# A two-layer MLA and Conformer MoE block: query copies on ScalarE, rotary sums on Pool, a negated maximum, and another order of the conv loads

## The chip, the cores and the metric

The kernel runs on one core of a Trainium2 chip. The metric is the device time of one execution in microseconds (us); with several executions it is their median. All data are float32 but for a few one-hot tables in bfloat16.

## The reference

Layer 0 mixes 512 latent tokens and 256 context tokens by latent attention with 16 heads, layer 1 by a Conformer convolution; each is followed by a mixture of 64 experts, 6 per token, plus a shared expert. Cut to what matters here:

```python
# layer 0: queries, 16 heads of 64 + 32 dims; the last 32 are rotated
q = (rmsnorm(h @ wq_a, q_norm) @ wq_b).reshape(B, L, 16, 96)
q_pe = v * cos + rot(v) * sin            # v = q[..., 64:]
s = einsum('bqhd,bkhd->bhqk', q, k) * 96 ** -0.5   # 768 keys
p = softmax(s)
x = x + g1 * (einsum('bhqk,bkhd->bqhd', p, v) @ wo)
x = x + g2 * moe(modulate(rmsnorm(x)))
# layer 1: conv
u = h @ pw1_w + pw1_b                    # 1024 -> 2048
u = a * sigmoid(g)                       # then 31 taps, layernorm, silu
x = x + g1 * (u @ pw2_w + pw2_b)
x = x + g2 * moe(modulate(rmsnorm(x)))
# both layers: shift, scale and gate of "modulate" are silu(c) @ mod_w
```

## The kernel before

The program is written out by hand for the engines, each with its own stream; semaphores are the only order between them. Tensors are held feature-major: 128 features on the partitions, tokens along the row. SBUF has a ring of four slots of 24 KB a partition for weights (`ring`), a tile `hT` of the same 24 KB for normalised activations, and `work`.

**Attention.** Heads go in 8 pairs (`m`), each pair in 8 blocks of 128 queries (`n`, with `i8 = n % 8`). For a block PE makes the scores (`scores`, L906) two blocks ahead of use, DVE takes their maximum over 768 keys (L1309) and multiplies it by minus the scale (L1311), ScalarE takes the exponential with that bias (L735) and sums it, DVE divides (L1315, L1317), PE transposes the result (`turn`, L916), and ScalarE (L353) and DVE (L355) copy it out of PSUM. DVE's copy of block n comes ahead of the division of block n+1. After the eighth block PE multiplies with V (L941). Between, PE projects the next pair in six parts (`project`): keys (L885), the two heads' queries (L889, parts 2 and 3 in blocks 2 and 3), values (L894, parts 4 and 5 in blocks 4 and 5). Part 4 reuses the PSUM bank of part 2, part 5 that of part 3. DVE empties the query banks in `q_out`, in blocks 3 and 4: a copy of 64 rows (L1296), two rotary products (L1297, L1298) and their sum (L1300). The order on DVE is that of the loop at L1320: divide, maximum of the next block, `q_out`, copy, and then, in five of eight blocks (1, 3, 4, 6 and 7), one mod block (L1228), which is a dot product of a row of the modulation weights, in `ring`, with silu(c), in `small`. Pool has no work during the attention: it clears a tile and issues two transfers of zeros to `y_rows` ahead of it (L537 to L541).

**MoE.** SP loads each expert's weights into a ring slot as soon as that slot's last user is done (`refill_up`, `refill_down`; `dn_ps` counts finished down products, the four shared ones first). One block of an expert with over 128 tokens is run as an extra block behind the 64 experts, once a layer, with its own load (L429). Then Pool gathers the results, 24 gathers of 128 rows of 4 KB (L530) into six buffers, and DVE adds them into the accumulator (L1535, `comb_used` counts). PE transposes the sums (L1143), the next norm follows, and the conv starts with PE's products with `pw1` (L1169). `pw1` lies in ring slots 0, 1 and two thirds of 2, `pw2` behind it. SP issues both loads at L453 and L454, once 20 gathered tiles are added.

## Time and profile before

| what | value |
|---|---|
| median of three timed runs | 2224.37 us (2222.91 to 2260.46) |
| profiled execution, its own time | 2243.39 us |
| its span, first to last instruction | 2241.0 us |
| mean granted TensorE clock | 0.932 of full |
| busy share PE, DVE, ScalarE, Pool | 83, 40, 20, 15% |
| attention | 134 to 445 us |
| MoE layer 0, experts | 540 to 1170 us |
| gathers and norm | 1170 to 1256 us |
| conv | 1256 to 1495 us |
| MoE layer 1 to the end | 1495 to 2241 us |

Busy shares are averages over stages of different kinds: the experts' stages wait for weights, the attention is a loop over three engines. What an edit is worth is read in its own stage, from the wait that ends last there. The page lists an engine's idle time with what ended it; a wait for several semaphores is put down to the last.

### The profile page before, as it was taken

How to read it: one execution, taken by the hardware profiler on the slowest of the kernel's cores; microseconds unless marked ns; L12 is line 12 of the kernel's file. 1: busy time of each engine (PE TensorE's matmuls, PEld its weight loads, DVE VectorE, ACT ScalarE, POOL GpSimd, SP SyncE). 2: the span in 40 equal slices, each digit the busy share in tenths (PEclk: the TensorE clock that was granted, in tenths of full speed). 3: DMA queues.
4: the chain of work that ended last, by engine and by line, in shares of the span. 5: the costliest groups of instructions: out<-in, count | busy, mean ns of one | idle time of the engine just before them, and what ended most of it. 6: DMA issues, size and time to landing. Idle time of an engine off the chain costs nothing.

```text
span 2241.0 us, 30677 instructions
## 1 busy us (share of the span) xinstructions
PE 1849.6 (83%) x9312; PEld 958.0 (43%) x9313; DVE 901.8 (40%) x1635; ACT 450.8 (20%) x807; POOL 346.2 (15%) x540
## 2 busy tenths in 40 slices
PE   5988989797999788887980898788989789988952
PEld 3444545444554444444440343344544445444521
DVE  1567777755422222222215489435322212221235
ACT  4133433303111111111110355321111111110102
POOL 0000000001011111111104078101111111111132
PEclk9999999998999999999995799799999999999985
DMA  9497221446699999999969200036899999999954
GB/s 391 162 366 309 76 76 38 188 150 277 243 409 398 408 393 397 397 402 394 390 215 358 101 1 0 0 128 246 308 399 406 395 394 411 400 398 392 379 192 161
DMA packets 94528, 624.56 MB, mean 279 GB/s; under 512 B 16000, under 2 KB 16128, under 8 KB 56704
## 3 DMA queue, kind: packets, MB, share of 16 engines
q1 hardware_dynamic: 43488, 499.18, 55.7%
q0 software_dynamic: 26112, 79.72, 9.8%
q10 hardware_dynamic: 24864, 44.84, 5.6%
q8 instruction: 36, 0.59, 0.1%
q14 instruction: 28, 0.23, 0.0%
HBM read 562.86 MB, written 76.28 MB: 285 GB/s over the span
## 4 chain that ended last, share of the span: by engine, by line
PE 54%; DMA 23%; DVE 9%; issue 4%; POOL 3%; ACT 2%; DVEq 0%; SPq 0%; ACTq 0%; POOLq 0%
DMA ring<-in 20%; PE PS L959 10%; PE PS L965 9%; PE PS L1169 5%; PE PS L972 5%; PE PS L986 4%; PE PS L997 3%; PE PS L1187 3%; PE PS L950 3%; PE PS L889 2%; POOL work L530 2%; PE PS L906 2%; PE PS L941 2%; PE PS L916 2%; DVE ring L1228 1%
## 5 line engine op out<-in xcount | busy, mean ns | idle before, releaser
L965 PE MATMUL PS<-ring,work 128*64 128x256 f32 x3360 | 414.1, 402 | 111.0 <-issue 108.2
L965 PEld LDWEIGHTS PS<-ring,work 128*64 128x64 f32 x3360 | 246.6, 144 | 254.3 <-issue 157.7
L1358 DVE TENSOR_TENSOR work<-work,PS 64x256 f32<-64x256 f32 x105 | 44.4, 423 | 518.5 <-ACT work L610 515.3
L972 PE MATMUL PS<-ring,work 128*64 128x512 f32 x840 | 203.3, 605 | 1.2 <-ACT work L636 0.7
L959 PE MATMUL PS<-ring,work 128*128 128x512 f32 x400 | 182.6, 611 | 19.5 <-issue 10.8
L1363 DVE COPY work<-PS 128x1024 f32<-128x1024 f32 x128 | 156.7, 1225 | 12.2 <-PE PS L997 2.2
L482 POOL COPY col_i<-idx 128x1 int32 (+1 forms) x128 | 23.2, 181 | 840.2 <-PE PS L997 825.5
L488 POOL DMA_INDIRECT work<-h_rows,col_i x128 | 124.7, 975 | 169.9 <-issue 169.9
L997 PE MATMUL PS<-cst,work 128*128 128x128 f32 x1040 | 140.8, 278 | 0.0
L610 ACT ACTIVATE work<-PS 64x256 f32<-64x256 f32 x105 | 39.5, 376 | 481.0 <-PE PS L965 481.0
L997 PEld LDWEIGHTS PS<-cst,work 128*128 128x128 f32 x1040 | 113.4, 141 | 53.4 <-issue 53.4
L1369 DVE COPY work<-PS 128x256 f32<-128x256 f32 x136 | 57.7, 424 | 181.2 <-PE PS L992 181.2
L959 PEld LDWEIGHTS PS<-ring,work 128*128 128x128 f32 x400 | 75.8, 194 | 110.5 <-issue 110.5
L986 PE MATMUL PS<-ring,work 128*128 128x512 f32 x264 | 119.2, 594 | 1.0 <-DVE work L1528 1.0
L554 POOL TENSOR_TENSOR work<-work 128x512 f32<-128x512 f32 x80 | 104.8, 1314 | 92.4 <-ACT work L760 83.0
L636 ACT ACTIVATE work<-PS 128x512 f32<-128x512 f32 x105 | 62.7, 597 | 268.9 <-PE PS L972 232.3
L1169 PE MATMUL PS<-hT,ring 128*128 128x512 f32 x256 | 114.1, 605 | 1.7 <-ACT hT L593 1.7
L1228 DVE SCALAR_TENSOR_TENSOR ring<-ring,small 128x1024 f32<-128x1024 f32 x80 | 95.5, 1219 | 36.4 <-DMA ring<-in 36.0
L1143 PE MATMUL PS<-cst,work 128*128 128x128 f32 x64 | 15.2, 389 | 110.4 <-DVE work L1535 110.4
L906 PE MATMUL PS<-work,hT 96*128 96x512 f32 (+1 forms) x256 | 96.4, 500 | 0.0
L1356 DVE TENSOR_TENSOR work<-work,PS 128x256 f32<-128x256 f32 x31 | 13.0, 419 | 197.3 <-ACT work L608 197.3
L972 PEld LDWEIGHTS PS<-ring,work 128*64 128x64 f32 x840 | 51.1, 136 | 79.2 <-issue 77.3
(233 smaller groups left out, 2145.8 us busy)
## 6 DMA issues: line engine op xcount, KB each, us to landing
ring<-in SPq DMA_DIRECT2D x155, 2048.0 KB, 17.2
ring<-in SPq DMA_DIRECT2D x130, 1024.0 KB, 17.7
y_rows<-sq POOLq DMA_DIRECT2D x2, 14336.0 KB, 61.4
y_rows<-work ACTq DMA_DIRECT2D x210, 128.0 KB, 9.1
ring<-in SPq DMA_DIRECT2D x3, 4096.0 KB, 14.7
y_rows<-work ACTq DMA_DIRECT2D x46, 256.0 KB, 9.8
ring<-in SPq DMA_DIRECT2D x2, 3072.0 KB, 12.4
h_rows<-work ACTq DMA_DIRECT2D x8, 512.0 KB, 15.8
```

The lines of the kernel that those rows point to most:

```text
L488: pool.indirect_dma_start(out=xg[n][0:p], out_offset=None, in_=h_rows[i], in_offset=bass.IndirectOffsetOnAxis(ap=col_i[0:p, n:n + 1], axis=0),
L554: nc.gpsimd.tensor_tensor(side[c % 2], before, tap_prod[n % 4], ALU.add).then_inc(side_add, 1)
L906: last = mm(bank(2 * (n % 2), 2)[:, c0:c0 + w], qT[m % 2][q][0:96, t * 128:(t + 1) * 128], kT[m % 2][q][0:96, c0:c0 + w], start=True, stop ...
L950: last = mm(bank(n % 2), wo_sb[:, c, n * 128:(n + 1) * 128], oT[:, c, :], start=(c == 0), stop=(c == DC - 1))
L959: last = mm(bank(6), lhs(c), w13(s)[:, :, c, :], start=(c == 0), stop=(c == DC - 1))
L965: last = mm(bank(6)[64 * q:64 * q + 64, 0:F], lhs(c)[:, 0:64], w13(s)[:, q, c, :], start=(c == 0), stop=(c == DC - 1), tile_position=(0, 6 ...
L972: last = mm(bank(4)[64 * q:64 * q + 64, :], actT[par][:, kk, 0:64], w2(s)[:, kk, q * 512:(q + 1) * 512], start=(kk == 0), stop=(kk == 1), ...
L986: last = mm(bank(4 + half), actT[par][:, kk, :], w2(s)[:, kk, half * 512:(half + 1) * 512], start=(kk == 0), stop=(kk == 1))
L997: last = tr(bank(1, 2)[:, c * 128:(c + 1) * 128], xg[par][:, c * 128:(c + 1) * 128], ident)
L1169: last = mm(bank(2 * (c % 2) + half), pw1_sb[:, kk, half * D + c * 128:half * D + (c + 1) * 128], hM[:, kk, :], start=(kk == 0), stop=(kk ...
L1228: last = V.scalar_tensor_tensor(mod_tile[at][:, j, :], mod_tile[at][:, j, :], 1.0, cs_row, ALU.mult, ALU.mult, accum_out=mod[i][:, part, c ...
L1363: V.tensor_copy(xgT[par].rearrange("p c t -> p (c t)"), bank(1, 2)).then_inc(xgT_ev, 1)
```

## The change

- `q_out` on DVE keeps only the two rotary products (new lines L1321 and L1322). The copy of the 64 plain rows goes to ScalarE (`q_copy`), after the exponentials of blocks 3 and 4, and multiplies by the softmax scale. The sum of the products goes to Pool, 16 times, and counts `q_ev`. The table of cosines and sines for queries is multiplied by the scale, so the exponential has none.
- The value projections wait for the products (`q_rope`) and the copy (`q_cp`), no longer for the sum; the scores wait for copy and sum. In the first pair ScalarE makes both query copies ahead of the value copies.
- The maximum is reduced with `negate=True` into the bias itself; the multiplication and its semaphore go.
- `pw1` is loaded in three parts: its share of slot 1 once expert 60 is done, that of slot 2 once expert 62 is done, that of slot 0, and then `pw2`, once all 24 gathers have landed. The extra expert block's weights go into `hT` and wait for no ring slot, in both layers.

```diff
+        SPARE = RING
+        def slot_ap(s):
+            return hT[:, :] if s == SPARE else ring[:, s * SLOT:(s + 1) * SLOT]
...
                     with nc.sync.Fori(0, many) as j:
-                        sp.wait_ge(m["dn_ps"], TT + E - 3)
                         sp.wait_ge(m["t_dn"], j + 1)
                         e = nc.sync.value_load(unit_i[0:1, ds(j, 1)], min_val=0, max_val=E - 1)
-                        expert(ds(e, 1), slot_of(E - 4), m["t_w"])
+                        expert(ds(e, 1), SPARE, m["t_w"])
...
-            sp.wait_ge(comb_used, TT * K - 4)
-            sp.dma_start(pw1_sb.rearrange("p c f -> p (c f)"), pw1).then_inc(pw_in, 16)
+            def load_pw1(k0, k1):
+                sp.dma_start(ring[:, k0 * 2 * D:k1 * 2 * D], pw1[:, k0 * 2 * D:k1 * 2 * D]).then_inc(pw_in, 16)
+            sp.wait_ge(M[0]["dn_ps"], TT + E - 3)
+            load_pw1(3, 6)
+            sp.wait_ge(M[0]["dn_ps"], TT + E - 1)
+            load_pw1(6, 8)
+            for n in range(6):
+                sp.wait_ge(comb_in[n], 16 * (TT * K // 6))
+            load_pw1(0, 3)
             sp.dma_start(pw2_sb.rearrange("p c f -> p (c f)"), pw2).then_inc(pw2_in, 16)
...
+            for n in range(H):
+                pool.wait_ge(q_rope, n + 1)
+                nc.gpsimd.tensor_tensor(qT[n // 2 % 2][n % 2][64:96, :], rope_t[0][64:96, :], rope_t[1][64:96, :], ALU.add).then_inc(q_ev, 1)
             moe(0)
...
+            def q_copy(m, q):
+                a.wait_ge(pj_ps, 6 * m + 3 + q)
+                A(qT[m % 2][q][0:64, :], bank(7 if q == 0 else 6)[0:64, :], ACT.Copy, scale=SM_SCALE).then_inc(q_cp, 1)
...
-                A(P[n % 2], bank(2 * (n % 2), 2)[:, 0:KEYS], ACT.Exp, bias=smx[:, n % 4, 1:2], scale=SM_SCALE,
+                A(P[n % 2], bank(2 * (n % 2), 2)[:, 0:KEYS], ACT.Exp, bias=smx[:, n % 4, 1:2],
                   accum_out=smx[:, n % 4, 2:3]).then_inc(exp_rdy, 1)
...
+                if m + 1 < NPAIR and i8 in (3, 4):
+                    q_copy(m + 1, i8 - 3)
...
-                elif part == 4:
-                    pe.wait_ge(q_ev, 2 * m + 1)
-                elif part == 5:
-                    pe.wait_ge(q_ev, 2 * m + 2)
+                elif part >= 4:
+                    pe.wait_ge(q_rope, 2 * m + part - 3)
+                    pe.wait_ge(q_cp, 2 * m + part - 3)
...
                 dve.wait_ge(pj_ps, 6 * m + 3 + q)
                 dve.wait_ge(q_ev, 2 * m + q)
-                dst = qT[m % 2][q]
-                V.tensor_copy(dst[0:64, :], b[0:64, :])
                 V.tensor_tensor(rope_t[0][64:96, :], b[64:96, :], k("rope")[64:96, :], ALU.mult)
                 V.tensor_tensor(rope_t[1][64:96, :], b[96:128, :], k("rope")[96:128, :], ALU.mult).then_inc(q_rope, 1)
-                dve.wait_ge(q_rope, 2 * m + q + 1)
-                V.tensor_tensor(dst[64:96, :], rope_t[0][64:96, :], rope_t[1][64:96, :], ALU.add).then_inc(q_ev, 1)
...
-                V.tensor_reduce(smx[:, n % 4, 0:1], bank(2 * (n % 2), 2)[:, 0:KEYS], AX.X, ALU.max).then_inc(max_rdy, 1)
-                dve.wait_ge(max_rdy, n + 1)
-                V.tensor_scalar(smx[:, n % 4, 1:2], smx[:, n % 4, 0:1], -SM_SCALE, None, ALU.mult).then_inc(nmax_rdy, 1)
+                V.tensor_reduce(smx[:, n % 4, 1:2], bank(2 * (n % 2), 2)[:, 0:KEYS], AX.X, ALU.max, negate=True).then_inc(nmax_rdy, 1)
```

The order on DVE in block 4 of the first pair, before: from the maximum of block 5 to the division of block 5 (`smx` holds maxima and sums, `PS` is PSUM, `hT` the queries, `ring` the products, P and the modulation weights).

```order
L1309 TENSOR_REDUCE smx<-PS 128x1 [waits p_rdy,s_ps]
L1311 TENSOR_SCALAR smx<-smx 128x1 [waits max_rdy]
L1296 COPY hT<-PS 64x512 [waits q_ev,pj_ps]
L1297 TENSOR_TENSOR ring<-PS,cst 32x512
L1298 TENSOR_TENSOR ring<-PS,cst 32x512
L1300 TENSOR_TENSOR hT<-ring 32x512 [waits q_rope]
L355 COPY work<-PS 128x2x128 [waits pT_ps]
L1228 SCALAR_TENSOR_TENSOR ring,mod<-ring,small 128x1024
L1315 RECIPROCAL smx<-smx 128x1 [waits exp_rdy]
L1317 TENSOR_SCALAR ring<-ring,smx 128x768 [waits den_rdy]
```

And with the change, where the file's later lines are some 20 further down:

```order
L1331 TENSOR_REDUCE smx<-PS 128x1 [waits p_rdy,s_ps]
L1321 TENSOR_TENSOR ring<-PS,cst 32x512 [waits q_ev,pj_ps]
L1322 TENSOR_TENSOR ring<-PS,cst 32x512
L360 COPY work<-PS 128x2x128 [waits pT_ps]
L1254 SCALAR_TENSOR_TENSOR ring,mod<-ring,small 128x1024
L1335 RECIPROCAL smx<-smx 128x1 [waits exp_rdy]
L1337 TENSOR_SCALAR ring<-ring,smx 128x768 [waits den_rdy]
```

Three instructions less stand between the maximum and the copy of P transposed; the mod block, which reads `ring` and `small`, is now the second instruction behind the last rotary product, whose semaphore starts Pool's sum.

SP's queue at the end of the first MoE layer, before: the extra block's two loads (ring), and the conv loads.

```order
L388 ISA
L388 DMA ring<-in 128x4096
L391 ISA
L391 DMA ring<-in 128x2048
L425 REGISTER_ALU
L425 COMPARE_AND_BRANCH
L424 UNCONDITIONAL_BRANCH
L453 DMA ring<-in 128x16384 [waits comb_used]
L454 DMA ring<-in 128x8192
```

And with the change:

```order
L393 ISA
L393 DMA hT<-in 128x4096
L396 ISA
L396 DMA hT<-in 128x2048
L430 REGISTER_ALU
L430 COMPARE_AND_BRANCH
L429 UNCONDITIONAL_BRANCH
L458 DMA ring<-in 128x6144 [waits dn_ps0]
L458 DMA ring<-in 128x4096 [waits dn_ps0]
L458 DMA ring<-in 128x6144 [waits comb_in3,comb_in4,comb_in2,comb_in5,comb_in1,comb_in0]
L467 DMA ring<-in 128x8192
```

The extra block's loads go to `hT`; `pw1` is split in three, and only its last part and `pw2` stand behind the wait for the gathers.

## Rows read from the trace of the kernel before

**Rows 1.** Busy time in two stretches: attention, end of the first MoE layer.
```profile
core 0: us, PE busy (x) PEld busy (x) DVE busy (x) ACT busy (x) POOL busy (x), PEclk, DMA share, GB/s
134.00:445.00 311.00, 269.92 (x1191) 154.99 (x1189) 230.35 (x470) 118.31 (x237) 0.00 (x0) 0.98 0.43 167
...
1170.00:1238.00 68.00, 4.96 (x14) 2.46 (x15) 31.60 (x26) 1.23 (x2) 27.13 (x25) 0.56 0.85 328
```

**Rows 2.** Chain of waits, attention: start, length, products with V of three pairs.
```profile
174.62 5.30 PE PS L941 x24
...
214.34 5.30 PE PS L941 x24
...
252.91 5.30 PE PS L941 x24
```

**Rows 3.** Stretches of 3 us, pair 3: the one of low clock.
```profile
283.00:286.00 3.00, 2.89 (x8) 1.89 (x9) 2.28 (x6) 1.75 (x4) 0.00 (x0) 0.55 0.00 0
```

**Rows 4.** Timeline, pair 2 between turn(4) and turn(7): start, length, engine, line.
```profile
239.22 0.68 DVE L1296 COPY hT<-PS 64x512 f32<-64x512 f32 x1
...
239.92 0.69 DVE L1297 TENSOR_TENSOR ring<-PS,cst 32x512 f32<-32x512 f32 x1
...
241.35 0.68 DVE L1300 TENSOR_TENSOR hT<-ring 32x512 f32<-32x512 f32 x1
242.07 0.42 DVE L355 COPY work<-PS 128x256 f32<-128x256 f32 x1
...
242.09 1.16 PE L894 MATMUL PS<-ring,work 128*128 128x128 f32 x8 [1.27 <-DVE hT L1300]
242.52 1.23 DVE L1228 SCALAR_TENSOR_TENSOR ring<-ring,small 128x1024 f32<-128x1024 f32 x1
...
244.54 0.88 PE L916 MATMUL PS<-cst,ring 128*128 128x128 f32 x6 [1.29 <-DVE ring L1317]
...
245.38 0.15 DVE L1311 TENSOR_SCALAR smx<-smx 128x1 f32<-128x1 f32 x1
...
250.74 0.88 PE L916 MATMUL PS<-cst,ring 128*128 128x128 f32 x6 [1.10 <-DVE ring L1317]
```

**Rows 5.** Lines L1576 and L554 (ns: shortest, median, longest), and Pool's run.
```profile
L1576 DVE TENSOR_TENSOR work<-work x8: 693/1673/1681, 1298.3 to 1411.8; 128x512 f32<-128x512 f32 x8
...
L554 POOL TENSOR_TENSOR work<-work x80: 1261/1272/1545, 1276.8 to 1409.2; 128x512 f32<-128x512 f32 x80
...
1295.49 5.57 POOL L554 TENSOR_TENSOR work<-work 128x512 f32<-128x512 f32 x4
```

**Rows 6.** Timeline, first pair: the wait ahead of its second V projection.
```profile
136.63 1.16 PE L894 MATMUL PS<-ring,work 128*128 128x128 f32 x8 [1.12 <-DVE hT L1300]
```

**Rows 7.** Timeline, last gathers of the first MoE layer and the conv loads.
```profile
1209.81 8.22 DVE L1535 SCALAR_TENSOR_TENSOR work<-work,small 128x1024 f32<-128x1024 f32 x6 [0.64 <-DMA work<-y_rows,row_i]
...
1212.22 1.07 POOL L530 DMA_INDIRECT work<-y_rows,row_i  x1 [0.30 <-issue]
1213.90 0.34 SPq L453 DMA_DIRECT2D ring<-in  x1
...
1235.84 1.28 DVE L1535 SCALAR_TENSOR_TENSOR work<-work,small 128x1024 f32<-128x1024 f32 x1 [17.81 <-DMA work<-y_rows,row_i]
...
1237.18 1.97 PE L1143 MATMUL PS<-cst,work 128*128 128x128 f32 x8 [62.14 <-DVE work L1535]
...
1256.82 5.46 PE L1169 MATMUL PS<-hT,ring 128*128 128x512 f32 x6 [1.72 <-ACT hT L593]
```

**Rows 8.** Line L530, all gathers of rows: issue to landing.
```profile
DMA to landing us min/median/max: 4.2/6.1/23.6
```

**Rows 9.** Timeline, second MoE layer: the same transposes.
```profile
2209.58 1.97 PE L1143 MATMUL PS<-cst,work 128*128 128x128 f32 x8 [48.28 <-DVE work L1535]
```

**Rows 10.** SP's queue: the last expert load and the extra block's.
```profile
1136.29 0.33 SPq L391 DMA_DIRECT2D ring<-in  x1
1143.89 0.35 SPq L388 DMA_DIRECT2D ring<-in  x1
```

More of the change, by code:

```diff
@@ L166, in build @@
         qT = [[hT[:, DC * T + (2 * a + b) * T:DC * T + (2 * a + b + 1) * T] for b in range(2)] for a in range(2)]
-        assert o[0] <= 12800
+        assert o[0] <= 12800 and DC * KEYS == SLOT
         hM = hT[:, 0:DC * T].rearrange("p (c t) -> p c t", c=DC)
@@ L220, in build @@
         rw_sb = hT[:, DC * T:DC * T + DC * E].rearrange("p (c e) -> p c e", c=DC)
+        SPARE = RING
+        def slot_ap(s):
+            return hT[:, :] if s == SPARE else ring[:, s * SLOT:(s + 1) * SLOT]
         def w13(s):
-            return ring[:, s * SLOT:s * SLOT + 2 * DC * F].rearrange("p (a c f) -> p a c f", a=2, c=DC)
+            return slot_ap(s)[:, 0:UP].rearrange("p (a c f) -> p a c f", a=2, c=DC)
         def w2(s):
-            return ring[:, s * SLOT + 2 * DC * F:(s + 1) * SLOT].rearrange("p (k d) -> p k d", k=2)
+            return slot_ap(s)[:, UP:SLOT].rearrange("p (k d) -> p k d", k=2)
         pw1_sb = ring[:, 0:DC * 2 * D].rearrange("p (c f) -> p c f", c=DC)
@@ L252, in build @@
         pj_ps, kv_ev, q_ev, q_rope = sem("pj_ps"), sem("kv_ev"), sem("q_ev"), sem("q_rope")
-        s_ps, max_rdy, nmax_rdy, exp_rdy, p_rdy, pT_ps, pT_act, pT_dve, o_ps, o_ev = (
-            sem(n) for n in ("s_ps", "max_rdy", "nmax_rdy", "exp_rdy", "p_rdy", "pT_ps", "pT_act", "pT_dve", "o_ps", "o_ev"))
+        s_ps, q_cp, nmax_rdy, exp_rdy, p_rdy, pT_ps, pT_act, pT_dve, o_ps, o_ev = (
+            sem(n) for n in ("s_ps", "q_cp", "nmax_rdy", "exp_rdy", "p_rdy", "pT_ps", "pT_act", "pT_dve", "o_ps", "o_ev"))
         wo_ps, wo_ev = sem("wo_ps"), sem("wo_ev")
@@ L386, in expert_up @@
                 def expert_up(e, s, done):
-                    sp.dma_start(ring[:, s * SLOT:s * SLOT + UP], exp_w[i, e, :, 0:UP].rearrange("o p n -> p (o n)")).then_inc(done, 16)
+                    sp.dma_start(slot_ap(s)[:, 0:UP], exp_w[i, e, :, 0:UP].rearrange("o p n -> p (o n)")).then_inc(done, 16)
                 def expert_down(e, s, done):
-                    sp.dma_start(ring[:, s * SLOT + UP:(s + 1) * SLOT], exp_w[i, e, :, UP:SLOT].rearrange("o p n -> p (o n)")).then_inc(done, 16)
+                    sp.dma_start(slot_ap(s)[:, UP:SLOT], exp_w[i, e, :, UP:SLOT].rearrange("o p n -> p (o n)")).then_inc(done, 16)
                 def expert(e, s, done):
@@ L726, in kv_out @@
                 last.then_inc(kv_ev, 1)
-            for part in (0, 1, 4, 5):
-                kv_out(0, part)
+            def q_copy(m, q):
+                a.wait_ge(pj_ps, 6 * m + 3 + q)
+                A(qT[m % 2][q][0:64, :], bank(7 if q == 0 else 6)[0:64, :], ACT.Copy, scale=SM_SCALE).then_inc(q_cp, 1)
+            kv_out(0, 0)
+            kv_out(0, 1)
+            q_copy(0, 0)
+            q_copy(0, 1)
+            kv_out(0, 4)
+            kv_out(0, 5)
             for n in range(NS):
@@ L901, in scores @@
                 pe.wait_ge(kv_ev, 4 * m + 2)
+                pe.wait_ge(q_cp, 2 * m + 1 + q)
                 pe.wait_ge(q_ev, 2 * m + 1 + q)
@@ L1130, in moe @@
                         pe.wait_ge(m["t_w"], j * 32 + 32)
-                        up_mm(lambda c: xgT[0][:, c, :], slot_of(E - 4)).then_inc(m["t_up"], 1)
+                        up_mm(lambda c: xgT[0][:, c, :], SPARE).then_inc(m["t_up"], 1)
                         pe.wait_ge(m["t_act"], j + 1)
@@ L1136, in moe @@
                         pe.wait_ge(m["y_ev"], TT + E)
-                        down_mm(0, slot_of(E - 4)).then_inc(m["t_dn"], 1)
+                        down_mm(0, SPARE).then_inc(m["t_dn"], 1)
                 pe.wait_ge(comb_used, TT * K + i * TT * K)
@@ L1150, in _ @@
             moe(0)
-            pe.wait_ge(pw_in, 16)
+            pe.wait_ge(pw_in, 48)
             def conv_taps(c):
@@ L1614, in constants @@
     cos, sin = np.cos(ang.astype(np.float32)), np.sin(ang.astype(np.float32)) * sign
-    put("rope", np.concatenate([cos, sin, cos, sin]))
+    put("rope", np.concatenate([cos, sin, cos * SM_SCALE, sin * SM_SCALE]))
     return c
```

## The prediction

> **What bounds the kernel now.** I read the chain that ended last first, since shares of busy time mix stages. Most of it is PE, and most of the transfers in it are expert weights, which the change leaves alone. So I look at two stretches only: the attention, where the chain runs over PE with short DVE pieces between, and the end of the first MoE layer.
>
> The table of stretches tells the two apart [rows 1]. In the attention, 134 to 445, PE is busy 269.92 of 311 us and DVE 230.35: neither fills it, so it is a loop of waits. In 1170 to 1238 PE is busy 4.96 of 68 us, while the DMA engines are at 0.85 of their time and move 328 GB/s: the stage waits for gathers.
>
> Pairs of heads are told apart by the starts of the product with V in the chain: 174.62, 214.34, 252.91, so 39.72 and 38.57 us [rows 2]. Every other pair holds some 3 us in which the granted clock is near the lower of its levels, as 0.55 in 283 to 286, after PE had waited twice [rows 3]; I take 38.57 as the undisturbed pair. Seven of the eight pairs also project the next pair and hold its two q_out calls.
>
> Inside a pair I follow turn (L916), which closes each block of 128 queries [rows 4]. In blocks 0 to 4 the projections keep PE full, and DVE waits for PE. After turn(4) it flips: DVE runs the second q_out (copy 239.22, first product 239.92, add 241.35), then the copy of P transposed at 242.07, a mod block at 242.52, and then the division. PE waits 1.27 us for the add before its last projection (242.09) and 1.29 us more before turn(5) at 244.54; turn(7) comes at 250.74.
>
> **The change part by part.** DVE's first q_out of a pair lies under four projection matmuls and is worth nothing. From the second goes the copy, 0.70 us from its start to the next start (239.22 to 239.92), and the add, 0.72 us (241.35 to 242.07) [rows 4]. The separate negation, 0.15 us long, stands between the maximum and the exponential or q_out; it goes as well: of it I count 0.1 us here. Together DVE reaches the copy of P transposed 1.5 us sooner. After turn(5) comes a block without a mod block, where the path is maximum, exponential, division, turn(6), and the negation is worth its 0.15 us [rows 4]. The two blocks behind it carry mod blocks and run round copy, mod block, division and turn; the negation is not in that loop, so nothing more. Sum without any new cost: 1.65 us a pair.
>
> ScalarE's new copies of 64x512 take about what the 64x512 copy takes on DVE, 0.68 us [rows 4]. Each stands behind the exponential of blocks 3 and 4 and ahead of a copy which waits for a turn behind the projection in any case; the projection that it reads is done before that turn. I cost it at nothing; were that cover gone, it is 0.68 us a call, and turn(5) would be late by it.
>
> The add on Pool is not in the trace. Its nearest row is Pool's 128x512 addition, 1.27 us, twice DVE's [rows 5]. Nobody waits for its result: the scores that read it stand in block 7, over 10 us later, and the projections now wait for the products and the copy. But it runs beside DVE, and a row speaks against that. DVE's L1576, an addition with both operands in SBUF, takes 0.693 us at its shortest and 1.673 at the median, and the first, at 1298.3, lies inside a run of Pool's additions [rows 5]: 0.98 us lost. The mod block L1228 also reads two SBUF tensors (ring and small), and in block 4 it is issued 0.45 us behind the copy that starts just as Pool starts. If it must wait for Pool's 1.27 us, it loses 1.27 - 0.45, some 0.9 us with the hand-over. In block 3 Pool is done before DVE has anything to issue.
>
> The bounds of this edit are thus 1.65 us (no wait) and 1.65 - 1.27 = 0.4 us (the whole addition lost). I take 1.65 - 0.9, rounded to 0.8 us a pair, since L1576 is the nearest row: same engine pair, same kinds of operands.
>
> The Trainium skill has a rule for it (SBUF — State Buffer, Who interferes with whom): a DVE instruction with two SBUF inputs and a GpSimd instruction that reads SBUF share a port pair, and the one that comes second is held for the whole of the other. By that rule it is 0.8 us a pair, without it 1.65; the trace agrees with the rule in L1576.
>
> Attention: 7 x 0.8 = 5.6 us. In the first pair the second V projection waited 1.12 us for the add until 136.63 [rows 6]; about 1.0 of it goes, as the products end 0.7 us sooner by the missing copy and the add is not waited for. The last pair has no projections; its three blocks without a mod block gain the negation, 3 x 0.15, some 0.4. Sum 7.0 us, bounds 4.2 and 13.0. PE's clock may gain or lose with the shorter gaps, the odd pairs' 1.1 us each; I leave that in the range.
>
> The reduction that negates is not in the trace. From below it can be what the reduction is now, which is my value: the same elements are read and one number written. From above see the third rival.
>
> The load order. Before, both conv weights are issued at 1213.90, when 20 of 24 gathered rows are added; the last gather was issued at 1212.22 [rows 7]. DVE is done with the others at 1209.81 + 8.22 = 1218.03 and then waits 17.81 us for that one gather, to 1235.84; PE starts at 1237.18. Any gather takes 6.1 us at the median to land, this one 23.6 [rows 8]: it shares the DMA engines with 12 MB. After the change nothing is issued until the gathers have landed, but for 5 MB of pw1 that go out when the experts 60 and 62 are done, at about 1144 and 1158, well before the first gather. So the last gather lands at 1212.22 + 1.07 + 6.1 = 1219.4, its addition takes 1.28, and PE starts at about 1220.8: 16.4 us sooner. The best case is DVE never waiting: 1218.03 + 1.34 = 1219.4, 17.8 us. The other end is the second layer, where no load stands behind the gathers: PE's idle time ahead of the same transposes is 48.28 us there and 62.14 here, so 13.9 us [rows 7, 9]. I take 16.
>
> Is the rest of the load in time? Slot 0's 3 MB and then pw2 are issued at 1219.4. At 328 GB/s [rows 1] 3 MB are 9.6 us, with 2 to 3 us of delay 1232. The first conv matmul stood at 1256.82 [rows 7], now about 1240.5: covered by 8 us. If the cover went because pw2 ran abreast, 7.3 MB at that rate land at 1242 to 1244, and it costs 2 to 3 us.
>
> SP's part in the tail: the extra block's weights now go into hT right behind expert 63's, at about 1136.6 and not 1143.89, and 3 MB of pw1 follow at 1143.9 [rows 10]. In this queue nothing stands behind them but each other; ScalarE's stores and Pool's last row gather run abreast. The gather is read only at 1160. I cost it at nothing.
>
> **Sum.** 7.0 + 16.0 = 23.0 us. The profiled execution took 2243.39 us for its span of 2241.0, so 2220.4 by its own time. It lies 0.9% above the timed median 2224.37, which is 1.4 above the lowest of the three; I carry the difference over to the median: 2201.4 us.
>
> **Rivals.** (a) Pool and DVE don't meet: 1.65 a pair, 11.6 + 1.4 = 13.0 us, 29 in all: 2195 us. For it: a 32-partition addition may be shorter than 1.27; against it the 0.98 us of L1576.
>
> (b) The early loads hold up the end of the first MoE layer. Expert 63's last MB (issued 1136.6) shares with 3 MB more, up to 9.6 us late against some slack, so 4; then the tail's gather and the last stores share with 5 MB of pw1, up to 9 more: 13 lost, 2214 us. For it: expert weights are still being issued at 1136, so the queues are not empty [rows 10]. Against it: the 5 MB are through by about 1166, ahead of the first gather.
>
> (c) Slower: the negated maximum takes a longer form. The price by blocks: three of eight blocks a pair are bound by DVE, all eight in the last pair, 7 x 3 + 8 = 29 reductions on the path. At twice the present length, 0.95 more each, that is 27.6 us lost against 23.0 won: 2229 us. It decides from 23.0 / 29 = 0.79 us extra a reduction. Nothing in the trace speaks for it but that no such row exists.
>
> (d) The loads change nothing: the last gather is late by itself, and only the 7 us of the attention stay, 2217 us. Against it: no gather of the second layer holds DVE more than about 1 us.
>
> **How the numbers follow.** The forecast 0.50, (a) 0.17, (b) 0.14, (c) 0.04, (d) 0.07, and 0.08 for what no row prices: the weight-bound MoE stages, which differ from one execution to the next (the three timed runs reach from 2222.91 to 2260.46). The range takes in (a) with four odd pairs freed of their clock dip and the best load case, 13.0 + 4.4 + 17.8 = 35, 2189, and 4 us of spread: 2185; above, (b) and (d) with a few us of spread: 2223. A change of 2%, 44.5 us, is about what a measurement of this kernel can tell from none. More than that to the good needs 2180, below the best case of every term: 0.07. Slower by over 2% needs (c) at well over double length or a disturbed stage: 0.03. Within 2%: 0.90.
>
> **What would show it.** In the profile after: pairs of about 37.8 us between V products; L1576-like lengthening of one mod block a pair, from 1.22 to about 2.1 us, in block 4 only; no wait of the V projection on DVE; the reduction still 0.95 us. At the first MoE layer's end PE's wait for the accumulation is shorter by 16 us, the last gather lands in about 6 us, and the first pw1 matmul waits for ScalarE, not for a transfer. Wrong: mod blocks unchanged and pairs of 36.9 say (a); PE waiting for expert 63 or for rows at 1150 to 1165 says (b); long reductions say (c); a DVE gap of over 10 us ahead of the last addition says (d).

## The result and the profile after

The changed kernel takes 2216.30 us, the median of 20 runs (2206.74 to 2220.51). The kernel before, run beside it, takes 2243.42 us over 20 runs (2217.74 to 2260.46), the three shown ahead of the prediction among them. The ratio is 0.9906, with a 95% interval of 0.988 to 0.9932: about 21 us faster, which by the bound of 2% counts as no change. The ratio leaves out a kernel's runs over 1.5% above its fastest; over all runs the medians lie 27.1 us apart and the means 23.7. The forecast time was 2201.4 us; the range (2185 to 2223) holds the result.

| | before | after |
|---|---|---|
| profiled execution, us | 2243.39 | 2219.18 |
| its span, us | 2241.0 | 2217.4 |
| last product with V of the attention starts | 437.40 | 426.59 |
| first MoE layer: PE starts on the gathered sums | 1237.18 | 1216.13 |
| second MoE layer: the same | 2209.58 | 2186.43 |
| spread of 20 runs, us | 42.7 | 13.8 |

So 10.8 us come from the attention, 10.2 more by the first MoE layer's end, and 2.1 between there and the second layer's end, which the change hardly touches.

The table of stretches for the changed kernel, after [rows 1] (us; then busy time and count for PE, PEld, DVE, ACT and POOL; PEclk, DMA share, GB/s):

```profile
134.00:445.00 311.00, 276.53 (x1213) 158.09 (x1212) 210.72 (x382) 127.21 (x253) 18.90 (x15) 0.98 0.43 167
1170.00:1218.00 48.00, 1.87 (x8) 1.57 (x8) 31.54 (x25) 0.20 (x1) 31.36 (x25) 0.51 0.82 289
```

DVE gave up 20 us of work in the attention, ScalarE took 9 and Pool 18.9. The wait for gathered rows is still the most idle stretch, now 48 us long.

The chain of waits, attention: start, length, the products with V of the first four pairs and the last two.

```profile
172.89 5.30 PE PS L967 x24
...
210.47 5.30 PE PS L967 x24
...
248.06 5.30 PE PS L967 x24
...
285.65 5.30 PE PS L967 x24
...
398.43 5.30 PE PS L967 x24
...
426.59 7.00 PE PS L967 x24
```

Every pair takes 37.59 us, where [rows 2] had 38.57 and 39.72 in turn. The 3 us of low clock of [rows 3], which began 9.6 us ahead of a product with V (292.58 in that trace), are gone; the stretch at that place of the pair now shows a granted clock of 1.00 (in the order of the table of stretches, PEclk behind POOL):

```profile
276.00:279.00 3.00, 1.52 (x8) 1.10 (x9) 2.67 (x6) 0.68 (x1) 0.00 (x0) 1.00 0.00 0
```

The timeline of pair 2 after the change, from the first block that sends work to Pool (3) to turn(5), against [rows 4] (start, length, engine, line, operation, tiles, count, and the wait before it):

```profile
230.33 1.26 POOL L557 TENSOR_TENSOR hT<-ring 32x512 f32<-32x512 f32 x1 [29.91 <-DVE ring L1322]
231.95 0.42 DVE L360 COPY work<-PS 128x256 f32<-128x256 f32 x1 [1.70 <-PE PS L942]
232.41 1.23 DVE L1254 SCALAR_TENSOR_TENSOR ring<-ring,small 128x1024 f32<-128x1024 f32 x1
...
236.70 0.42 DVE L360 COPY work<-PS 128x256 f32<-128x256 f32 x1
236.75 1.26 POOL L557 TENSOR_TENSOR hT<-ring 32x512 f32<-32x512 f32 x1 [5.16 <-DVE ring L1322]
236.78 1.10 PE L919 MATMUL PS<-ring,work 128*128 128x128 f32 x8
237.16 1.93 DVE L1254 SCALAR_TENSOR_TENSOR ring<-ring,small 128x1024 f32<-128x1024 f32 x1
239.21 0.62 DVE L1337 TENSOR_SCALAR ring<-ring,smx 128x768 f32<-128x768 f32 x1
239.74 0.95 DVE L1331 TENSOR_REDUCE smx<-PS 128x1 f32<-128x768 f32 x1
239.88 0.87 PE L942 MATMUL PS<-cst,ring 128*128 128x128 f32 x6 [2.00 <-DVE ring L1337]
```

In block 3 Pool is through by 231.59, before DVE starts, and the mod block takes 1.23 us. In block 4 the mod block is issued 0.41 us behind Pool's start and takes 1.93 us: 0.71 longer, with its end as if it had begun at 237.87, just ahead of Pool's end at 238.01. The V projection (L919) waits for nothing. The reduction that negates takes 0.95 us, as the plain one did.

The timeline at the end of the first MoE layer after the change, against [rows 7]: the last additions, SP's loads, the transposes, and the first conv matmul.

```profile
1213.40 2.67 DVE L1555 SCALAR_TENSOR_TENSOR work<-work,small 128x1024 f32<-128x1024 f32 x2 [0.41 <-DMA work<-y_rows,row_i]
1214.83 0.33 SPq L458 DMA_DIRECT2D ring<-in  x1
1215.21 0.43 SPq L467 DMA_DIRECT2D ring<-in  x1
1216.13 1.97 PE L1169 MATMUL PS<-cst,work 128*128 128x128 f32 x8 [48.30 <-DVE work L1555]
...
1235.95 2.90 PE L1195 MATMUL PS<-hT,ring 128*128 128x512 f32 x3 [1.72 <-ACT hT L609]
```

None of the additions from 1210 on waits longer than 0.64 us, PE waits 48.30 us and not 62.14, and the conv's first matmul waits for ScalarE, 1.72 us as before. The line of the gathers, after [rows 8]:

```profile
DMA to landing us min/median/max: 4.3/5.8/6.5
```

What the prediction did not price stands in the tail of the same layer (timeline of the changed kernel): ScalarE's copies of a result wait for the store of an earlier one, and PE for them.

```profile
1145.17 0.60 ACT L652 ACTIVATE work<-PS 128x512 f32<-128x512 f32 x1 [4.95 <-DMA y_rows<-work]
...
1149.84 0.60 ACT L652 ACTIVATE work<-PS 128x512 f32<-128x512 f32 x1 [1.45 <-DMA y_rows<-work]
...
1150.58 1.94 PE L998 MATMUL PS<-ring,work 128*64 128x512 f32 x8 [1.25 <-ACT work L652]
...
1158.43 0.60 ACT L652 ACTIVATE work<-PS 128x512 f32<-128x512 f32 x1 [7.99 <-DMA y_rows<-work]
```

Here the stores are under way together with 5 MB of `pw1`; whether that is the cause is tried below (e11).

### The profile page after: what moved, and what is told of

Read it like the earlier page. It is cut to its first block, busy times and chain, and to the rows that moved or that the text cites. A ratio compares the mean times of both kernels' runs of the same rounds, so it can differ in the third digit from the quotient of the medians.

```text
span 2217.4 us, 30694 instructions
## 1 busy us (share of the span) xinstructions
PE 1846.7 (83%) x9312; PEld 957.4 (43%) x9313; DVE 877.6 (40%) x1539; ACT 459.9 (21%) x823; POOL 371.9 (17%) x556
## 4 chain that ended last, share of the span: by engine, by line
PE 55%; DMA 22%; DVE 8%; issue 4%; POOL 3%; ACT 2%; ACTq 0%; DVEq 0%; SPq 0%; POOLq 0%
DMA ring<-in 20%; PE PS L985 10%; PE PS L991 9%; PE PS L1195 5%; PE PS L1012 5%; PE PS L998 4%; PE PS L1023 3%; POOL work L543 3%; PE PS L914 3%; PE PS L1213 3%; PE PS L976 3%; PE PS L967 2%; PE PS L942 2%; DMA y_rows<-work 2%; PE PS L932 2%
## 5 line engine op out<-in xcount | busy, mean ns | idle before, releaser
L991 PE MATMUL PS<-ring,work 128*64 128x256 f32 x3360 | 422.7, 409 | 113.9 <-issue 111.2
L985 PE MATMUL PS<-ring,work 128*128 128x512 f32 x368 | 163.4, 597 | 11.7 <-issue 7.8
L626 ACT ACTIVATE work<-PS 64x256 f32<-64x256 f32 x105 | 39.4, 375 | 491.3 <-PE PS L991 489.0
L1254 DVE SCALAR_TENSOR_TENSOR ring<-ring,small 128x1024 f32<-128x1024 f32 x80 | 100.6, 1281 | 36.4 <-DMA ring<-in 35.9
L1012 PE MATMUL PS<-ring,work 128*128 128x512 f32 x248 | 111.8, 594 | 0.0
L985 PEld LDWEIGHTS PS<-ring,work 128*128 128x128 f32 x368 | 68.2, 190 | 92.4 <-issue 92.4
L1169 PE MATMUL PS<-cst,work 128*128 128x128 f32 x64 | 14.9, 385 | 96.7 <-DVE work L1555 96.7
```

What stands on the lines that cost most here:

```text
L985: last = mm(bank(6), lhs(c), w13(s)[:, :, c, :], start=(c == 0), stop=(c == DC - 1))
L991: last = mm(bank(6)[64 * q:64 * q + 64, 0:F], lhs(c)[:, 0:64], w13(s)[:, q, c, :], start=(c == 0), stop=(c == DC - 1), tile_position=(0, 6 ...
L1012: last = mm(bank(4 + half), actT[par][:, kk, :], w2(s)[:, kk, half * 512:(half + 1) * 512], start=(kk == 0), stop=(kk == 1))
L1254: last = V.scalar_tensor_tensor(mod_tile[at][:, j, :], mod_tile[at][:, j, :], 1.0, cs_row, ALU.mult, ALU.mult, accum_out=mod[i][:, part, c ...
```

## The experiments

For each kernel I read three stretches of its timeline: pair to pair in the attention; the tail, from the up products of the next-to-last expert of the first layer to the first gather's issue; and the gather stage, from there to PE's transposes. In the profiled executions, in us:

| kernel | pairs | tail | gather stage | slowest gather |
|---|---|---|---|---|
| before | 38.6 to 39.7 | 34.7 | 57.8 | 23.6 |
| after | 37.59 | 36.1 | 44.0 | 6.5 |
| changed kernel again (e14) | 37.59 | 40.3 | 40.9 | 6.8 |
| loads alone (e1) | 38.6 to 40.2 | 38.5 | 41.3 | 6.7 |
| attention alone (e2) | 37.59 | 34.6 | 39.9 | 6.7 |
| later `pw1` parts (e11) | 37.6 to 38.7 | 35.4 | 44.6 | 6.8 |
| before, loads at 18 added (e12) | 38.6 to 40.1 | 34.7 | 70.7 | 35.4 |
| before, loads at 24 added (e13) | 38.6 to 40.3 | 34.7 | 40.2 | 6.5 |

In the second layer of all these kernels, with no load near, the tail is 34.6 to 34.9 and the gather stage 40.1 to 44.7. So the gather stage by itself differs by some 4 us from one execution to the next, and the tail hardly at all.

**The loads alone (e1).** The kernel before, with the load order and the extra block in `hT` of the change, and nothing of the attention.

```diff
-                        sp.wait_ge(m["dn_ps"], TT + E - 3)
...
-                        expert(ds(e, 1), slot_of(E - 4), m["t_w"])
+                        expert(ds(e, 1), SPARE, m["t_w"])
...
-            sp.wait_ge(comb_used, TT * K - 4)
-            sp.dma_start(pw1_sb.rearrange("p c f -> p (c f)"), pw1).then_inc(pw_in, 16)
...
+            sp.wait_ge(M[0]["dn_ps"], TT + E - 3)
+            load_pw1(3, 6)
+            sp.wait_ge(M[0]["dn_ps"], TT + E - 1)
+            load_pw1(6, 8)
+            for n in range(6):
+                sp.wait_ge(comb_in[n], 16 * (TT * K // 6))
+            load_pw1(0, 3)
```

> The load order alone, on the kernel before (pw1 in three parts, the extra block's weights in hT). My theory: the attention stays at pairs of 38.6 and 39.7 us; no gather lands later than about 7 us; PE's idle time ahead of the transposes of the first MoE layer falls from 62 to about 48 us, of which up to 1.5 us is given back before it, because ScalarE's stores and the pw1 parts share the DMA engines. Sum 12 to 14 us faster than before. Rival: the load order carries the whole 21 us and the attention's gain is eaten by the weight-bound experts: then this run is 20 us or more faster. Second rival: the early parts cost as much as they bring: within 4 us of before.

Measured: 2228.80 us, median of 12 (2220.62 to 2237.40), against 2234.74 of the kernel before: ratio 0.9977 (0.9949 to 1.0006). The profile shows the 16 us shorter wait, yet the median moves by some 5 us. A gain that a profile shows in full and the runs show in part needed another theory.

**The attention alone (e2).** The changed kernel with the loads and ring slots of before.

```diff
-            sp.wait_ge(M[0]["dn_ps"], TT + E - 3)
-            load_pw1(3, 6)
-            sp.wait_ge(M[0]["dn_ps"], TT + E - 1)
-            load_pw1(6, 8)
...
+            sp.wait_ge(comb_used, TT * K - 4)
+            sp.dma_start(pw1_sb.rearrange("p c f -> p (c f)"), pw1).then_inc(pw_in, 16)
```

> The attention's edits alone, with the loads as before. My theory: pairs of 37.6 us without a clock dip, the last product with V 10 to 11 us sooner; the last gather of the first MoE layer still waits 17 to 24 us behind pw1 and pw2. Of the 10.8 us the experts' stage keeps about 2, so 8 to 9 us faster than before. Rival: the experts' stage is bound by its weights and absorbs all of it: within 2 us of before.

Measured: median 2218.61 us of 12, ratio 0.994 (0.990 to 0.9979), and runs from 2208.19 to 2248.88, so more than the 8 to 9 us expected. In the profiled one, at 2208.25, the wait that the change is meant to remove isn't there, though this kernel has the old loads. Its timeline, the last gather's issue, the loads, the transposes:

```profile
1199.16 1.07 POOL L531 DMA_INDIRECT work<-y_rows,row_i  x1 [0.30 <-issue]
...
1201.22 0.34 SPq L454 DMA_DIRECT2D ring<-in  x1
...
1206.81 1.97 PE L1157 MATMUL PS<-cst,work 128*128 128x128 f32 x8 [44.23 <-DVE work L1543]
```

The loads are issued 0.99 us behind the end of the last gather's issue, where [rows 7] had 1213.90 - 1213.29 = 0.61 us. The new theory: the kernel before is a mixture. In some executions the loads catch the last gather (it lands some 17 us late), in others it gets away. Its own 20 runs fit: twelve lie at 2242.96 or above, with a mean of 2248, eight at 2236.26 or below, with a mean of 2225. The gap between the two groups isn't always there: of the 23 runs of the kernel before that stand beside e1 and e2, five lie in it (2236.53 to 2242.26). So the time of a single run does not tell its kind.

**Loads a little earlier, and behind the gathers (e12, e13).** The kernel before with one number changed, so that its loads should catch the gathers always, or never.

```diff
-            sp.wait_ge(comb_used, TT * K - 4)
+            sp.wait_ge(comb_used, TT * K - 6)
```

(e12; e13 has `TT * K`.)

> The kernel before with one number changed: pw1 and pw2 are issued when 18 gathered tiles are added, not 20. My theory now: before is a mixture; when the loads are issued, the last gather is either already in the DMA queues or stands behind 8 to 12 MB, and that costs 16 to 18 us. With 18, two or three gathers are still to be issued, so every execution pays: no run below about 2238 us, a median 15 us above the lower runs of before, the longest gather 20 us or more in every profile. Rival: the slow runs of before come from something else in the chip; then this kernel has the same spread as before, 2220 to 2255.

> The kernel before with one number changed: pw1 and pw2 are issued when all 24 gathered tiles are added. No gather can stand behind them, so by my theory no run is slow: PE's transposes 40 to 44 us behind the first gather in every execution. pw1, now whole at that point, lands 24 us later, some 4 us after the first conv matmul could start, so it costs about 4 us against the lower runs of before: all runs in 2222 to 2235 us, the median 5 to 8 us below the median of before. Rival as in the run with 18: the spread stays at 30 us.

Measured: e12 takes 2252.14 us, median of 10, all between 2248.04 and 2259.47; ratio 1.0091 (1.0054 to 1.0127). Its timeline: the loads, the last gather's issue, and the last three additions, which wait for one gather each.

```profile
1214.08 0.34 SPq L453 DMA_DIRECT2D ring<-in  x1
...
1215.18 1.08 POOL L530 DMA_INDIRECT work<-y_rows,row_i  x1 [0.30 <-issue]
...
1235.66 1.28 DVE L1535 SCALAR_TENSOR_TENSOR work<-work,small 128x1024 f32<-128x1024 f32 x1 [17.07 <-DMA work<-y_rows,row_i]
1247.87 1.29 DVE L1535 SCALAR_TENSOR_TENSOR work<-work,small 128x1024 f32<-128x1024 f32 x1 [10.92 <-DMA work<-y_rows,row_i]
1250.57 1.28 DVE L1535 SCALAR_TENSOR_TENSOR work<-work,small 128x1024 f32<-128x1024 f32 x1 [1.42 <-DMA work<-y_rows,row_i]
...
1251.91 1.97 PE L1143 MATMUL PS<-cst,work 128*128 128x128 f32 x8 [74.97 <-DVE work L1535]
```

e13 takes 2228.99 us, median of 12, all between 2224.02 and 2235.97; ratio 0.9948 (0.9914 to 0.9982). Its timeline: the transposes, and the first conv matmul with its weight load, which waits for the transfer of `pw1`.

```profile
1222.92 1.97 PE L1143 MATMUL PS<-cst,work 128*128 128x128 f32 x8 [44.53 <-DVE work L1535]
...
1246.58 0.50 PEld L1169 LDWEIGHTS PS<-hT,ring 128*128 128x128 f32 x2 [6.09 <-DMA ring<-in]
1246.58 3.78 PE L1169 MATMUL PS<-hT,ring 128*128 128x512 f32 x4 [5.79 <-ACT hT L593]
```

The matmul waits 5.79 us and not 1.72, so it is 4.1 us late. One number moves all runs to the long side or all to the short one, and the spread falls to 11.4 and 12.0 us, where the kernel before, run beside them, has 39.1. So it is the order of loads and gathers that makes the spread. How many gathers a long run of the kernel before has caught isn't shown: one such execution has a trace, with one caught, and e12 catches three.

**The changed kernel again, and its early parts later (e14, e11).** e14 is the changed kernel once more. e11 issues both early parts of `pw1` only when all experts' down products are done.

```diff
-            sp.wait_ge(M[0]["dn_ps"], TT + E - 3)
+            sp.wait_ge(M[0]["dn_ps"], TT + E)
             load_pw1(3, 6)
-            sp.wait_ge(M[0]["dn_ps"], TT + E - 1)
             load_pw1(6, 8)
```

> The changed kernel once more, beside the next run on one chip. By my theory its ratio to before depends on how many executions of before caught the last gather: 0.988 to 0.994, its own runs within 15 us; pairs of 37.59 us; 36 to 39 us from the last two experts to the first gather. Rival: the pairs or that stretch differ from one execution to the next as much as between the kernels.

> The changed kernel with pw1's two early parts issued once the last of the 64 experts is done, and nothing else. If these parts hold up ScalarE's stores and the extra block, the stretch from the last two experts to the first gather falls to 34.6 to 35.7 us, 2 to 4 us less than in the changed kernel, and so does the median. Rival: the 36 to 39 us come from the extra block's weights being issued 7 us sooner, which is still so here; then the stretch stays at 36 or more.

Measured: e14 2212.68 us (2205.55 to 2215.42, 6 runs), e11 2211.36 us (2207.38 to 2220.86, 6 runs). The tail of e14 is longer than the 36 to 39 us expected. It falls from 40.3 to 35.4 us, nearly what it is without early parts: they cost it 5 us in that execution. The extra block's weights still go out early in e11, so it isn't they that hold the tail up. The timeline of e14 shows where:

```profile
1140.83 0.60 ACT L652 ACTIVATE work<-PS 128x512 f32<-128x512 f32 x1 [5.49 <-DMA y_rows<-work]
...
1147.50 3.68 PE L998 MATMUL PS<-ring,work 128*64 128x512 f32 x8 [2.50 <-ACT work L652]
...
1154.46 0.60 ACT L652 ACTIVATE work<-PS 128x512 f32<-128x512 f32 x1 [7.10 <-DMA y_rows<-work]
```

The time does not follow: the medians differ by 1.3 us, within both spreads. In e11's profile the gather stage takes 44.6 us, where the changed kernel's two executions have 44.0 and 40.9, and three pairs of its attention have a stretch of low clock (38.3 to 38.7 us). Whether the 5 MB, then nearer to the gathers, make them longer, I can't say: the second layer's stage reaches 44.7 with nothing beside it. Tail and gather stage together take 80.0 us in e11, and 80.1 and 81.2 in the changed kernel's two executions. All ten executions with parts issued ahead of the gathers have 78.1 to 81.2, the two without them and without a caught gather (e2, e13) 74.5 and 74.9. That looks as if moving the parts later only moved the loss; but the second layers, with no load near, reach from 74.6 to 79.6. So the hold-up is real in the tail; what it costs in the end stays open.

**The sum back on DVE (e6).**

```diff
-            for n in range(H):
-                pool.wait_ge(q_rope, n + 1)
-                nc.gpsimd.tensor_tensor(qT[n // 2 % 2][n % 2][64:96, :], rope_t[0][64:96, :], rope_t[1][64:96, :], ALU.add).then_inc(q_ev, 1)
...
+                dve.wait_ge(q_rope, 2 * m + q + 1)
+                V.tensor_tensor(qT[m % 2][q][64:96, :], rope_t[0][64:96, :], rope_t[1][64:96, :], ALU.add).then_inc(q_ev, 1)
```

> The changed kernel with the rotary sum back on DVE, behind the two products; Pool has none. DVE does the sum itself, 0.72 us, but its mod block in block 4 no longer waits for Pool, 0.71 us: the two cancel, pairs of 37.6 us again. Rival: handing the sum to Pool is worth its 0.72 us in full, and the pair is 38.3 us here; or, if the wait for the port is more than it looks, below 37.4.

Measured: one run, 2207.26 us, and pairs of 37.59 us, the same within a hundredth or two. Its timeline in block 4:

```profile
233.53 0.68 DVE L1321 TENSOR_TENSOR hT<-ring 32x512 f32<-32x512 f32 x1
234.24 0.42 DVE L360 COPY work<-PS 128x256 f32<-128x256 f32 x1
234.70 1.23 DVE L1251 SCALAR_TENSOR_TENSOR ring<-ring,small 128x1024 f32<-128x1024 f32 x1
...
236.72 0.87 PE L939 MATMUL PS<-cst,ring 128*128 128x128 f32 x6 [2.01 <-DVE ring L1336]
```

DVE spends 0.71 us on the sum, to the next start, and the mod block is 0.70 us shorter. The move to Pool is worth nothing.

**The sum on Pool twice (e5).** The second is issued behind the first and writes the same; the scores, and DVE's next pair of products, wait for both.

```diff
+                pool.wait_ge(q_ev, 2 * n + 1)
+                nc.gpsimd.tensor_tensor(qT[n // 2 % 2][n % 2][64:96, :], rope_t[0][64:96, :], rope_t[1][64:96, :], ALU.add).then_inc(q_ev, 1)
```

> The changed kernel with Pool's sum made twice (the second into the same rows, behind the first). If the mod block of block 4 waits for Pool, it now waits for both: about 3.2 us long, or 1.9 us and then the division long, and turn(5) comes about 1.3 us later; pairs of 38.9 us for 37.6. Rival: the 1.93 us are not Pool's; then the mod block stays at 1.93 and the pair at 37.6.

Measured: one run, 2230.14 us. Four of the six pairs take 40.5 us, two 39.8 and 39.5. The timeline in block 4:

```profile
239.42 1.26 POOL L557 TENSOR_TENSOR hT<-ring 32x512 f32<-32x512 f32 x1 [4.20 <-DVE ring L1324]
239.82 1.93 DVE L1256 SCALAR_TENSOR_TENSOR ring<-ring,small 128x1024 f32<-128x1024 f32 x1
240.75 2.12 POOL L559 TENSOR_TENSOR hT<-ring 32x512 f32<-32x512 f32 x1
...
241.88 1.42 DVE L1339 TENSOR_SCALAR ring<-ring,smx 128x768 f32<-128x768 f32 x1
...
243.35 1.54 PE L944 MATMUL PS<-cst,ring 128*128 128x128 f32 x6 [2.80 <-DVE ring L1339]
```

The two engines hold each other in turn: Pool's first the mod block (+0.7 us), the mod block Pool's second (2.12 for 1.26), that one the division (1.42 for 0.62). Nothing else differs, so this is the meeting of the two engines. The pairs lost 2.9 us and not the 1.3 expected. Counted from the last product with V, turn(5) comes 1.2 us later than in the changed kernel, as expected. The rest goes with the clock: the transposes behind the division take 1.54 us and not 0.87, and from 244 to 248 us the granted clock is 0.50, where the changed kernel has 1.00.

**The negation back (e7).**

```diff
-                V.tensor_reduce(smx[:, n % 4, 1:2], bank(2 * (n % 2), 2)[:, 0:KEYS], AX.X, ALU.max, negate=True).then_inc(nmax_rdy, 1)
+                link(V.tensor_reduce(smx[:, n % 4, 0:1], bank(2 * (n % 2), 2)[:, 0:KEYS], AX.X, ALU.max))
+                V.tensor_scalar(smx[:, n % 4, 1:2], smx[:, n % 4, 0:1], -1.0, None, ALU.mult).then_inc(nmax_rdy, 1)
```

> The changed kernel with the maximum negated by an instruction of its own again (by -1, the scale being in the queries). By my sum it is worth 0.1 us in block 4 and 0.15 in block 5: pairs of 37.84 us, and no difference in the last pair, where before and the changed kernel took 28.1 us each. Rival: it is worth 0.15 in every block that DVE bounds, 38.2 us a pair.

Measured: one run, 2221.41 us. Undisturbed pairs take 37.98 us, so 0.39 more, where I had counted 0.25; the last pair 28.8 and not 28.1. In three pairs a stretch of low clock is back (38.6 to 39.4 us). The line of the negation:

```profile
L1332 DVE TENSOR_SCALAR smx<-smx x64: 153/154/154, 137.5 to 426.5; 128x1 f32<-128x1 f32 x64
```

**Mod blocks elsewhere (e3, e4).** What binds block 4 on DVE is the mod block; the first blocks of a pair are bound by PE. e3 moves the one of block 4 to block 2, beside none there; e4 puts them in blocks 0, 1, 2 (two) and 3.

```diff
-                for b in range(n * ATTN_BLOCKS // NS, (n + 1) * ATTN_BLOCKS // NS):
+                BEFORE = (0, 0, 1, 2, 3, 3, 3, 4, 5)
+                for b in range(5 * m + BEFORE[i8], 5 * m + BEFORE[i8 + 1]):
```

(e4: `(0, 1, 2, 4, 5, 5, 5, 5, 5)`.)

> The changed kernel with one mod block a pair moved from block 4 to block 2 (same number a pair). If the 1.93 us of the mod block in block 4 is a wait for Pool's sum (port contention), all mod blocks now take 1.22 us, since Pool's sum meets only copies out of PSUM, and turn(5) comes 1.9 us sooner: 1.2 for the mod block itself, 0.7 for the lost wait; pairs of 35.7 us, the attention 13 us shorter, 10 to 13 us in all. Rival: the lengthening belongs to block 4 whatever runs there; then the division that now follows the copy is long (its 128x768 product over 1.3 us for 0.62), and a pair gains 1.2 us, not 1.9.

> The changed kernel with the five mod blocks of a pair in blocks 0, 1, 2, 2 and 3, where PE is full and DVE waits. Beyond the run with one moved block, turn(7) also comes about 0.5 us sooner (the loop of copy, mod block, division and turn, 3.27 us, gives way to that of maximum, exponential and division, about 2.8). Pairs of 35.2 us, the attention 16 to 17 us shorter than in the changed kernel, 2200 us in all or a little over. Rival: the second mod block of block 2 or the one of block 0 makes DVE late for turn(2) or turn(1); then a pair stays at 35.7 us or more and this run is no better than the one with one moved block.

Measured: e3 2206.76 us (4 runs, 2203.94 to 2210.04), ratio 0.9864 (0.9803 to 0.9925), pairs of 36.19. Half a microsecond of what I expected is missing, and its timeline in block 4 shows it:

```profile
231.77 1.26 POOL L557 TENSOR_TENSOR hT<-ring 32x512 f32<-32x512 f32 x1 [4.24 <-DVE ring L1322]
...
232.38 1.07 DVE L1337 TENSOR_SCALAR ring<-ring,smx 128x768 f32<-128x768 f32 x1
```

With the mod block gone, the division meets Pool's sum and takes 1.07 us for 0.62. e4: 2210.13 us (6 runs), pairs of 36.77 and a last pair of 30.8 instead of 28.2, where pairs of 35.2 were expected: the rival came true, and this is no better than e3. I put it down to the two mod blocks in one block, above all where nothing is projected; that was not tried by itself, and the last pair also has 6 us at a granted clock of 0.50 to 0.55 (408 to 414) ahead of its product with V.

**Two mod blocks moved (e10).** Mod blocks in blocks 0, 1, 2, 3 and 7, with e11's later parts.

```diff
+                BEFORE = (0, 1, 2, 3, 4, 4, 4, 4, 5)
```

> The changed kernel with the mod blocks of a pair in blocks 0, 1, 2, 3 and 7, and with pw1's two early parts issued once the last of the 64 experts is done, under the extra block. From the runs so far: a pair is 36.2 us with block 4 free of a mod block; with block 6 free too turn(7) comes 0.5 us sooner, 35.7 us a pair. From the last two experts to the first gather it took 34.6 us with the late loads and 36.1 to 39.1 with the early ones; here 34.6 to 35.5, since the 5 MB pass in the 15 us of the extra block. Transposes 40 to 44 us behind the first gather. In all about 12 to 16 us faster than the changed kernel, 2201 to 2205 us. Rival: the loads collide with the extra block's own store or with the first gathers, and the gathers' stage grows by 5 us or more.

Measured: 2197.93 us, median of 6 (2195.01 to 2200.18), against 2238.82 of the kernel before: ratio 0.9797 (0.9745 to 0.985), so whether the gain is 2% is unclear. It is below the 2201 to 2205 expected. Tail and gather stage take 35.7 and 44.1 us. The chain of waits, two of its products with V:

```profile
203.94 5.30 PE PS L966 x24
...
239.61 5.30 PE PS L966 x24
```

Pairs of 35.67 us and a last pair of 28.1; the last product with V starts at 410.35, 16.2 us sooner than in the changed kernel, and the median is 14.8 below e14's, though the two ran beside different runs of the kernel before (medians 2238.82 and 2235.62).

## Why the prediction was right or wrong

**The pair: right.** Forecast 0.8 us, measured 38.57 - 37.59 = 0.98. DVE reached the copy of P transposed sooner, the V projection's wait went, and the path flipped onto the mod block, as the rows of block 4 show. The meeting with Pool cost 0.71 us for 0.9. By the Trainium skill (SBUF — State Buffer, Who interferes with whom) the second instruction waits for the whole of the first; here that would be 238.01 - 237.16 = 0.85, so the trace agrees to within 0.14 us. My 0.9 was some 0.2 too much, part of it the hand-over that I had added. Rival (a), pairs of 36.9, is refuted by the row of 1.93 and by e5. And e6 adds what the sum had hidden: with 0.68 us back on DVE and the meeting gone the pair is the same, so the gain is the copy's and the negation's. e7 prices the negation at 0.39, above my 0.25; the copy to ScalarE was not undone by itself.

**First pair and last pair.** In the two profiled executions the first product with V came 1.73 us sooner, where 1.0 and the first pair's 0.8 were forecast. That fit is luck: this start differs from one execution to the next by more. With the old attention it is at 174.62, 172.89 (e1), 173.92 (e12) and 174.07 (e13), with the new one at 172.89, 172.83 (e14), 170.61 (e2) and 168.91 (e11). Between the last two products with V nothing seems gained (28.16 us after 28.10) for my 0.4. But 28.10 is the shortest of the old attention's: e1, e12 and e13 have 28.8, 28.6 and 28.4, and e7, with the negation back, 28.8, while e2, e11 and e14 have 28.2 like the changed kernel. So some 0.3 of my 0.4 is there, and one execution hid it.

**The clock.** I had left the dips in the range at 1.1 us each; three of them went (39.72, 39.67 and 39.57 us against 38.57), 3.2 us. The changed kernel has one of its own in the first pair (a granted clock of 0.60 from 163 to 166 us), where the kernel before has none; its price is inside the 1.73. Attention: 1.73 + 6 x 0.98 + 3.2 = 10.8 us, for my 7.0. In the pairs behind the first, dips are seen again in e5, e7 and e11, and not in e3, e4, e6 and e10. In e5 and e7 DVE holds PE up for longer than in the changed kernel, but e11's attention is that of the changed kernel, word for word. Why they come and go is open.

**The loads: mechanism right, taken as always there.** The wait of 17.81 us is gone, the last gather lands in 6 us, PE waits 13.8 us less and starts on the conv without waiting for `pw1`. Forecast 16 us of 13.9 to 17.8; the low end, taken from the second layer's 48.28, was the right row: with the last gather free, the stage is as long as that layer's.

**The base and the sum.** What failed is the step after: "I carry the difference over to the median". The profiled execution, 2243.39 us, was one in which the loads caught the last gather; the median that I subtracted from, 2224.37, was, to judge by its time, one in which they did not. e12 and e13 show that both kinds exist, and that the moment of the loads decides between them. From an execution of the second kind the loads' term is nothing, and rival (d)'s sum, 7 us and 2217, is what that base gives; measured were 2216.30. So the result lies 14.9 us above the forecast and within the range only because the range reached up to rivals (b) and (d), neither of which is what put it there: that is luck. From the profiled one, 23.0 us gave 2220.4; its counterpart took 2219.18. The base was wrong: of 20 runs of before the median is 2243.42. The sum was near, in part by luck. Between the two profiled executions the attention gave 10.8 us for 7.0 and the gather stage 13.8 for 16; the tail lost 1.3, the experts between attention and tail 2.3, and from the first layer's transposes to the end 3.2 were won, none of which was in the sum. The last two are no more than executions differ by: from the last product with V to the tail it is 707.2 us before and 709.5 after, and 704.6 (e14) to 710.4 (e13) elsewhere; from the transposes to the end 1006.2 and 1003.1, and 1000.1 (e14) to 1008.0 (e11) elsewhere. I had seen that "the three timed runs reach from 2222.91 to 2260.46" and put it down to the MoE stages.

**SP's part in the tail: "I cost it at nothing".** That was wrong, and rival (b) true in small: 1.3 us in the profiled execution, 5.6 in e14's, and 3.7 in e1's, against 13 forecast for (b). The other kernels with early parts (e3 to e7) have tails of 37.9 to 39.5 us, so 3.2 to 4.8 more than before; the profiled one is the mildest. It is not expert 63's weights that were late but the stores of results, under way together with `pw1`, and through them ScalarE and PE.

So e1's small gain has an account, as an estimate. e13's mean, 2228.9 us, less the 4.1 of its late load is 2224.8 for executions without a caught gather. The 23 runs of the kernel before beside e1 have a mean of 2234.7, so catching costs them 9.9 on average, which is 0.56 of the 17.6 us of one caught gather (62.14 less e13's 44.53). Less 3.7 in the tail some 6 are left; measured 5, with an interval of -1 to 11.

**The reduction: right.** It takes 0.95 us with the negation; rival (c) is refuted.

## What to carry to other kernels

Before subtracting a gain read from one profile, look which of the timed runs that profile resembles: a spread of 40 us in 2240 was a second kind of execution here, and a small transfer issued just ahead of a large one is where to look for it. A small operation handed to Pool won nothing here, since DVE then worked on SBUF tensors beside it; compare the length of the instruction behind, not the one moved. Filler work belongs in blocks in which another engine is the bound: moving two of a pair's five mod blocks won 16 us on top of the 11 of all the edits of the attention here.

## What the runs showed of the hardware that was not expected

- Whether a gather is caught by 12 MB of loads hangs on tenths of a microsecond: caught with 0.61 us between its issue and theirs (23.6 us to land), free with 0.99 (6.7 at most). In e12 the third gather from the end, again 0.61 us ahead of the loads, is caught too (its addition waits until 23.3 us behind its issue). These are three gathers in three executions; where the edge lies was not measured.
- With three gathers caught (e12), the last, issued 1.1 us behind the first load, took 35.4 us to land, against a median of 6.1 and the 23.6 of the single one in the kernel before.
- Pool is held by DVE as DVE is by Pool: the second sum in e5 took 2.12 us for 1.26. In five meetings (three in e5, one each in e3 and the changed kernel) the held one ended 0.14 to 0.20 us sooner than if it had begun when the other ended.
- A sum over 32 partitions x 512 takes Pool 1.26 us, as long as one over 128 partitions (1.27).
- The gather stage, the same instructions, took 40.0 to 44.7 us in the second layer of different executions. The cause is open.
